# PEER values: dense products with V replaced by one row gather per token and slot

## The reference, cut to what matters

```python
def block(xb):
    ...
    sv, si = lax.top_k(s, PEER_TOPK)
    ...
    e = (i1 * PEER_NKEYS + i2).reshape(T, PEER_HEADS * PEER_TOPK)
    gate = jax.nn.softmax(cv, axis=-1).reshape(T, PEER_HEADS * PEER_TOPK)
    act = jax.nn.gelu(jnp.einsum('ted,td->te', u_tab[e], xb).astype(jnp.float32))
    coef = (gate * act).astype(xb.dtype)
    return jnp.einsum('te,ted->td', coef, v_tab[e])
```

## Time and profile before

| what | us |
|---|---|
| median of three runs | 5477.62 |
| span of the profiled execution | 5473.6 |
| TensorE busy | 5015.2 (92%) |
| VectorE busy | 2899.3 (53%) |
| ScalarE busy | 1068.2 (20%) |
| GpSimd busy | 455.4 (8%) |
| moved by DMA | 476.12 MB, mean 87 GB/s |

### The profile page before, as it was taken

How to read it: one execution, slowest core, us unless ns; L and a number is a source line. 1 busy time by engine, 2 the same in 40 slices (tenths; PEclk the granted TensorE clock), 3 DMA queues, 4 the chain that set the end, 5 groups by cost and what they waited for, 6 DMA issues and landing times. The chain is left out here.

```text
span 5473.6 us, 76074 instructions
## 1 busy us (share of the span) xinstructions
PE 5015.2 (92%) x26871; PEld 4496.7 (82%) x26871; DVE 2899.3 (53%) x7212; ACT 1068.2 (20%) x1825; POOL 455.4 (8%) x328
## 2 busy tenths in 40 slices
PE   7999889998798999988887699999999999999996
PEld 6757888884598999988887688888888899889886
DVE  1021733333315999877776566666644444444444
ACT  2111111111311222222222211111111121112111
POOL 0000033430000000000000022222200000000000
PEclk9999589999799999999989899999999999999998
DMA  3100300002222233244445533333321221121122
GB/s 114 39 23 16 129 23 1 1 1 85 96 70 79 100 105 110 77 134 131 136 131 144 154 141 140 142 142 133 141 76 57 72 72 59 61 72 64 56 72 81
DMA packets 450919, 476.12 MB, mean 87 GB/s; under 512 B 311344, under 2 KB 376240, under 8 KB 449328
## 3 DMA queue, kind: packets, MB, share of 16 engines
q1 hardware_dynamic: 136240, 354.12, 18.6%
q10 hardware_dynamic: 307728, 91.43, 6.2%
q0 software_dynamic: 6768, 28.32, 1.4%
HBM read 336.45 MB, written 137.36 MB: 87 GB/s over the span
## 5 line engine op out<-in xcount | busy, mean ns | idle before, releaser
L1752 DVE TENSOR_TENSOR peer_y<-peer_y,stored_pv 128x512 f32<-128x512 f32 x648 | 443.0, 686 | 271.1 <-PE stored_pv L1781 270.3
L1779 PE MATMUL stored_pv<-stored_Vh,stored_Ch 128*128 128x512 f32 x1296 | 505.5, 390 | 33.1 <-DVE stored_Cl L1738 33.1
L1780 PE MATMUL stored_pv<-stored_Vl,stored_Ch 128*128 128x512 f32 x1296 | 505.2, 390 | 0.0
L1781 PE MATMUL stored_pv<-stored_Vh,stored_Cl 128*128 128x512 f32 x1296 | 505.1, 390 | 0.0
L1952 DVE TENSOR_TENSOR peer_y<-peer_y,experts_pv 128x512 f32<-128x512 f32 x504 | 341.8, 687 | 286.1 <-PE experts_pv L1992 286.1
L1975 PE MATMUL experts_pu<-peer_xh,experts_Uh 128*128 128x384 f32 x1344 | 450.5, 335 | 7.0 <-DVE experts_Ul L1918 7.0
L1977 PE MATMUL experts_pu<-peer_xh,experts_Ul 128*128 128x384 f32 x1344 | 450.2, 335 | 0.0
L1976 PE MATMUL experts_pu<-peer_xl,experts_Uh 128*128 128x384 f32 x1344 | 450.2, 335 | 0.0
L1990 PE MATMUL experts_pv<-experts_Vh,experts_Ch 128*128 128x512 f32 x1008 | 396.1, 393 | 15.1 <-DVE peer_y L1952 12.7
L1599 DVE TENSOR_SCALAR gates_scaled<-gates_iota,retrieve_slotT 128x128 f32<-128x128 f32 x1152 | 396.2, 344 | 0.0
L1991 PE MATMUL experts_pv<-experts_Vl,experts_Ch 128*128 128x512 f32 x1008 | 393.7, 391 | 0.0
(11 more groups left out here) (297 smaller groups left out, 9408.9 us busy)
## 6 DMA issues: line engine op xcount, KB each, us to landing
gates<-gates_G ACTq DMA_DIRECT2D x72, 1024.0 KB, 11.0
stored_C<-acts SPq DMA_DIRECT2D x72, 576.0 KB, 3.8
stored_G<-gates SPq DMA_DIRECT2D x72, 576.0 KB, 4.8
stored_Vr<-in_peer_v SPq DMA_DIRECT2D x72, 512.0 KB, 6.4
experts_G<-gates SPq DMA_DIRECT2D x56, 576.0 KB, 3.8
experts_Ur<-in_peer_u SPq DMA_DIRECT2D x56, 512.0 KB, 5.7
experts_Vr<-in_peer_v SPq DMA_DIRECT2D x56, 512.0 KB, 5.9
acts<-topk_act SPq DMA_DIRECT2D x135, 192.0 KB, 1.9
```

What stands on the lines that cost most here:

```text
L1752: nc.vector.tensor_tensor(dst, dst, pv[r % RING][:], ALU.add).then_inc(y_added, 1)
L1779: mm(pv[r % RING][:], Ch[p][j][:, t], Vh[p][j][:, cols], start=(j == 0), stop=False)
L1780: mm(pv[r % RING][:], Ch[p][j][:, t], Vl[p][j][:, cols], start=False, stop=False)
L1781: last = mm(pv[r % RING][:], Cl[p][j][:, t], Vh[p][j][:, cols], start=False, stop=(j == 1))
```

## The change

The change keeps the picking of experts and makes the activations as before, for all tokens and all 128 blocks: 54 of them in stage_topk (TOPK_AHEAD is 6), and 74 in a new stage, stage_rest, which does nothing else. Each block's activations are stored tile by tile, as nine [128 x 128] pieces, in nine DRAM tensors acts0 to acts8, one word for each expert and token. Gates are no longer spread, and stage_gates, stage_stored and stage_experts go.

A new stage, stage_values, works token by token. It turns the slots of each tile so that a token is a partition, and computes for each token and slot the row of V and the word of its activation. GpSimd then issues, for each of 9 tiles and 128 slots, an indirect DMA that brings one activation for each of 128 tokens (line 1634) and an indirect DMA that brings one row of V of 4 KB for each of 128 tokens (line 1641), into a ring of 12 buffers. The words of a tile are fetched one tile ahead, in turn with the rows. VectorE multiplies activations with gates (line 1674) and adds coefficient times row onto four running sums (lines 1683 and 1686), which it joins at a tile's end (lines 1689 to 1692). At the start of each of tiles 1 to 7 GpSimd waits until VectorE has used all rows issued so far (line 1653). Line numbers here are those of the changed kernel.

```diff
@@ class Ahead
     def store(self, sp, n):
         for c in range(NTC):
             sp.wait_ge(self.gelu_done, 3 * n + (c + 4))
-            sp.dma_start(self.dram["acts"][n + self.first][:, c * TC:(c + 1) * TC], self.act[c][:]).then_inc(self.act_out[c], 16)
+            for t in range(TC // P):
+                dst = self.dram[f"cells{c * (TC // P) + t}"][n + self.first]
+                sp.dma_start(dst, self.act[c][:, t * P:(t + 1) * P]).then_inc(self.act_out[c], 16)
...
-TOPK_AHEAD = 5
-GATE_AHEAD = 3
+TOPK_AHEAD = 6
...
@@ stage_topk, VectorE
-                    if half == 0:
-                        ahead.low(dve, t * A + 4, 4)
+                    ahead.low(dve, t * A + 4 + half, 4 + half)
...
-def stage_gates(core, xh, xl):
...
+def stage_rest(core, xh, xl, first):
+
+    nc = core.nc
+    R = 2
+    LEFT = P - first
...
+        @block.sync
+        def _(sp):
+            ahead.load(sp, 0)
+            with sp.Fori(0, LEFT // R - 1) as i:
+                for b in range(R):
+                    ahead.load(sp, i * R + (b + 1))
+                    ahead.store(sp, i * R + b)
...
         @block.tensor
         def _(pe):
             ahead.begin(pe=pe)
...
+            with pe.Fori(0, LEFT // R) as i:
+                for b in range(R):
+                    for c in range(NTC):
+                        ahead.products(pe, i * R + b, b, c)
...
+def stage_values(core, y):
...
+    RING = 12
+    SUMS = 4
...
+            def gather_act(i, k):
+                pool.indirect_dma_start(act[i % 2][:, k:k + 1], None, dram[f"acts{i}"],
+                                        bass.IndirectOffsetOnAxis(ap=cell[:, i, k:k + 1], axis=0)).then_inc(act_in[i % 2], 16)
+
+            def gather_row(i, k):
+                n = i * SLOTS + k
+                if n >= RING:
+                    pool.wait_ge(v_used, n - RING + 1)
+                pool.indirect_dma_start(V[n % RING][:], None, dram["peer_v"],
+                                        bass.IndirectOffsetOnAxis(ap=row[:, i, k:k + 1], axis=0)).then_inc(v_in[n % RING], 16)
...
+            pool.wait_ge(turned_read, 3)
+            for k in range(SLOTS):
+                gather_act(0, k)
+            for i in range(TILES):
+                if i + 1 < TILES:
+                    pool.wait_ge(turned_read, 3 * (i + 2))
+                    if i >= 1:
+                        pool.wait_ge(v_used, i * SLOTS)
+                for k in range(SLOTS):
+                    if i + 1 < TILES:
+                        gather_act(i + 1, k)
+                    gather_row(i, k)
...
+            for i in range(TILES):
+                dve.wait_ge(act_in[i % 2], 16 * SLOTS * (i // 2 + 1))
+                a = act[i % 2]
+                v.tensor_tensor(a[:], a[:], gate[:, i, :], ALU.mult).then_inc(coef_done, 1)
...
+                for k in range(SLOTS):
+                    n = i * SLOTS + k
+                    total = sums[k % SUMS]
+                    dve.wait_ge(v_in[n % RING], 16 * (n // RING + 1))
+                    if k < SUMS:
+                        v.tensor_scalar(total[:], V[n % RING][:], a[:, k:k + 1], None, ALU.mult).then_inc(v_used, 1)
+                    else:
+                        dve.wait_ge(v_used, n - SUMS + 1)
+                        v.scalar_tensor_tensor(out=total[:], in0=V[n % RING][:], scalar=a[:, k:k + 1], in1=total[:],
+                                               op0=ALU.mult, op1=ALU.add).then_inc(v_used, 1)
+                dve.wait_ge(v_used, (i + 1) * SLOTS)
+                v.tensor_tensor(sums[0][:], sums[0][:], sums[1][:], ALU.add).then_inc(joined, 1)
+                v.tensor_tensor(sums[2][:], sums[2][:], sums[3][:], ALU.add).then_inc(joined, 1)
+                dve.wait_ge(joined, 3 * i + 2)
+                v.tensor_tensor(y[:, i, :], sums[0][:], sums[2][:], ALU.add).then_inc(joined, 1)
...
@@ build
                 stage_topk(core, xh, xl)
-                stage_gates(core, xh, xl)
+                stage_rest(core, xh, xl, TILES * TOPK_AHEAD)
             y = pr.sb("y", [P, TILES, D])
-            made = TILES * (TOPK_AHEAD + GATE_AHEAD)
-            stage_stored(core, y, made)
-            stage_experts(core, xh, xl, y, made)
+            stage_values(core, y)
             stage_final(core, y)
```

More of the change, by code:

```diff
@@ L1552, in _ @@
             turn(TILES - 1)
-def stage_gates(core, xh, xl):
-    nc, dram = core.nc, core.dram
[L1561 to L1578, removed]
+def stage_rest(core, xh, xl, first):
+    nc = core.nc
+    R = 2
+    LEFT = P - first
+    with Stage(core, "rest") as st:
+        ahead = Ahead(core, st, R, first, xh, xl)
+        block = st.block()
+        @block.sync
[5 more added lines that the diff above has]
+                    ahead.store(sp, i * R + b)
+            ahead.load(sp, LEFT - 1)
+            ahead.store(sp, LEFT - 2)
+            ahead.store(sp, LEFT - 1)
+            ahead.stored(sp, LEFT)
+        @block.scalar
+        def _(act):
+            ahead.begin(act=act)
+            ahead.high(act, 0, 0)
+            with act.Fori(0, LEFT // R - 1) as i:
+                for b in range(R):
+                    ahead.high(act, i * R + (b + 1), (b + 1) % R)
+                    ahead.gelu(act, i * R + b)
+            ahead.high(act, LEFT - 1, 1)
+            ahead.gelu(act, LEFT - 2)
+            ahead.gelu(act, LEFT - 1)
+        @block.vector
+        def _(dve):
+            ahead.begin(dve=dve)
+            with dve.Fori(0, LEFT // R) as i:
+                for b in range(R):
+                    ahead.low(dve, i * R + b, b)
+        @block.tensor
+        def _(pe):
+            ahead.begin(pe=pe)
+            with pe.Fori(0, LEFT // R) as i:
+                for b in range(R):
+                    for c in range(NTC):
+                        ahead.products(pe, i * R + b, b, c)
@@ new lines, in stage_values @@
+def stage_values(core, y):
+    nc, dram = core.nc, core.dram
+    RING = 12
+    SUMS = 4
+    with Stage(core, "values") as st:
+        lane = st.sb("lane", [P, 1])
+        expert = st.sb("expert", [P, T])
+        row = st.sb("row", [P, TILES, SLOTS], U32)
+        cell = st.sb("cell", [P, TILES, SLOTS], U32)
+        gate = st.sb("gate", [P, TILES, SLOTS])
+        act = [st.sb(f"act{i}", [P, SLOTS]) for i in range(2)]
+        V = [st.sb(f"V{i}", [P, D]) for i in range(RING)]
+        sums = [st.sb(f"sum{i}", [P, D]) for i in range(SUMS)]
+        pt = [st.psum(f"pt{i}", [P, 2, P]) for i in range(2)]
+        lane_done = st.sem("lane_done")
+        experts_made = st.sem("experts_made")
+        turned, turned_read = st.sem("turned"), st.sem("turned_read")
+        act_in = [st.sem(f"act_in{i}") for i in range(2)]
+        v_in = [st.sem(f"v_in{i}") for i in range(RING)]
+        coef_done = st.sem("coef_done")
+        v_used = st.sem("v_used")
+        joined = st.sem("joined")
@@ L1586, in _ @@
         @block.vector
         def _(dve):
[L1588 to L1600, removed]
+            v = nc.vector
@@ L1602, in _ @@
         @block.tensor
         def _(pe):
[L1604 to L1617, removed]
```

375 lines of the change are left out of this document (36 added, 339 removed).

## The result

The changed kernel takes 6627.19 us (median of four runs, 6620.42 to 6641.75) against 5477.17 us for the kernel before: ratio 1.211 with an interval of 1.209 to 1.212, 21% slower. I had forecast 6210 us, 13% slower. The direction came out as written, and so did the engine that sets the pace, GpSimd; one term of the sum, its price for a gather, was 0.2 us too small, and it stands there 2304 times.

The account below looks back on a forecast made before the run. TensorE bounds the kernel before; in the new stage GpSimd's gathers would set the pace. Dense products and start to 3381 us, plus 2782 us of gathers, plus 45 us last stage: 6208 us, forecast 6210 us, range 5300 to 7200.

Parts of the forecast that it names:

- Dense part: Picking and rest stages: 128 blocks of U at 12.87 us each, 1647 us from 1717.2, ending at 3364.6 us.
- The third rival: Dense stages: nine stores a block break the 12.87 us; losing 3 us a block gives 6590 us; chance 0.05.
- the cover that I named for the nine stores: Dense stages: SyncE issues nine stores and one load in 3.3 of 12.87 us a block, so it has room.
- The price of a gather: Values stage: each indirect DMA holds GpSimd 1.17 us, 2304 of them 2696 us; chance 0.62.
- The second rival: Values stage: GpSimd's gathers and VectorE shut each other out, 3.48 us a slot, 7480 us in all; chance 0.13.
- The first rival: Values stage: gathers cost GpSimd 0.575 us like direct DMAs, the DMA engines set the pace, 5438 us; chance 0.20.
- The DMA engines: Last tile of the values stage: 128 row gathers at 1.50 us (350 GB/s) instead of 1.17 add 42 us.
- The boundaries: Values stage: at seven tile boundaries GpSimd waits for VectorE to use up the tile before, 33 us together.
- the end: After the last gather: last landing and three joins 7 us, then the last stage 45 us.
- the signs that I had listed: Values stage: GpSimd almost gapless, gathers near 1.2 us, line 1686 at 1.3 us and half idle, DMA share about 0.7.

Follow-up runs that it names:

- the phases: Changed kernel with its values stage replaced by four phases of back-to-back gathers (words or rows, 128 or 64 tokens), pauses between, computation with V left out: 5373.44 us.
- sums in PSUM: Changed kernel with three running sums in PSUM instead of four in SBUF: 6621.47 us, ratio to the kernel before 1.2095.
- the run with fewer tokens: Changed kernel with the first tile's word gathers over 128, 64, 32 and 16 tokens and direct DMAs for the last tile's rows: 6595.71 us, single run.

## Why the prediction came out as it did

The sum against the profiled execution of the changed kernel, 6633 us, 423 us above the forecast:

- **Dense part.** 12.87 us a block held in the picking stage (12.84) and was generous in the stage with nothing beside it (12.50). The last dense product starts at 3343 us instead of ending at 3365, and the first gather at 3350.5 instead of 3384.5: -34 us. The third rival is out; the cover that I named for the nine stores was there.
- **The price of a gather**, the term that was too small: 1.17 us. From the first gather to the last start are 3215 us; less 38 us at seven boundaries that is 1.38 us a gather, and 3177 - 2304 x 1.17 = +482 us. I had built it from a direct DMA plus two passes over 128 indices at 2.32 ns a value. The parts were wrong one by one: an index costs 1 ns, the fixed part is 0.82 us instead of 0.54, and there is a gap of 0.30 us that a direct DMA doesn't have. That they add up to 1.25, close by, is luck. The rest, 0.13, is VectorE's hold.
- **The two limits.** In the changed kernel the hold alone makes the mean gather 1.075 us long, 1.38 from start to start, since 860 of its 861 long gathers are held ones. The second limit doesn't come into play: by the account of the phases, against 1.40 us a gather, the lead is 18 us at most in the first two tiles, 14 from there to the last tile and 23 at its end, and the slow pace needs 27 (sums in PSUM) to 30 (phases). With the hold removed the second limit alone gives 6621 us; that this is nearly the same time looks like chance. In the run with fewer tokens, where the first tile was cheaper, both show: 126 of its 934 gathers over 1.0 us are not held ones. At 6371 us it had issued 2176, and (6371 - 3352) / 1.40 = 2156, a lead of 20 gathers, 27 us; the direct DMAs behind were slowed for 27 us.
- **The second rival** was half right, in a way that I had put inside the range ("some tenths of a us a gather"): the hold exists, falls on GpSimd alone, and ends with VectorE's instruction. The Trainium skill has the rule in "SBUF — State Buffer", section "SBUF: two separate sides" (VectorE with two SBUF inputs and a GpSimd operation that reads SBUF share a pair of ports, one at a time). For gathers the traces agree, with 0.94 us against up to 2.0, and 0.95 again with the sums in PSUM; that a gather which starts first holds VectorE in turn, as the rule has it, the trace doesn't show: 1022 of line 1686's instructions start inside a gather and take 1283 to 1287 ns.
- **The first rival** decided below 0.85 us a gather. Nothing here came near it, since even 16 tokens cost 1.14.
- **The DMA engines.** I took 350 GB/s and added 42 us for the last tile; it ran at 404 GB/s and the term was not there: -42 us.

```profile
6411.00:6566.00 155.00, 0.00 (x0) 0.00 (x0) 150.49 (x120) 0.00 (x0) 118.44 (x121) 0.50 1.02 404
```

- **The boundaries** cost 38 us instead of 33, 7 times and at most 5.6 us, as worked out, and the end 66 us instead of 52. -34 + 482 - 42 + 5 + 14 = 425, of 423.

```profile
POOL values_act L1634 <- DVE values_sum L1686: 38.1, 7, 5.6
```

Of the signs that I had listed, line 1686 at 1.28 us and idle half the time and a DMA share of 0.63 against 0.7 came out. GpSimd is never free, but it isn't busy almost without a gap: 2476.8 of 3230 us, 77%, with 0.30 us behind each gather; and lines 1634 and 1641 take 1.00 and 1.15 us on average instead of near 1.2 both.

What stays open is what the second limit is. That gathers slow to 1.40 us whatever their tokens and bytes once a lead of 27 to 30 us is used up, that a pause gives it back, and that their data land as soon as before all the same, is shown; what stands behind it no run here tells.

## What to carry to other kernels

Price a gather by its count: here 1.25 us of GpSimd for each, 1.38 on average beside VectorE instructions with two inputs in SBUF, 1.40 where more than some 150 to 220 follow each other without a pause, and almost nothing for its bytes or its tokens, so bring everything that a token needs in one gather. With 8 KB for both rows instead of a word and a row, the time from the first gather to the last falls from 3215 to 2899 us, although VectorE does two instructions a slot there; the other 1137 of the 1449 us less come from the dense products left out, since gathers begin at 2214 us instead of 3350.5. When a wait is taken away and the time stays, compare the pace in the first microseconds of the stage with that in its middle; a second limit that needs time to fill shows only there. And an engine that looks idle by nature, like GpSimd at 8% before, has to be priced for each instruction that a change hands to it.

## What the hardware showed unexpectedly

- Gathers slow to 1.40 us each after 153 to 216 in a row, though the last of 400 words had landed 1.42 us after its gather's end; direct DMAs that follow are slowed for 27 us, while direct DMAs alone run at 0.55 us, 600 in a row.
- GpSimd's gather waits for VectorE's instructions with two SBUF inputs, 0.94 us becoming up to 2.0, and VectorE never for a gather (1287 ns at most in 1022); a direct DMA from the same engine doesn't wait (537 ns median, 606 at most, 116 of the 128 started inside such an instruction).
- One core gathered rows at random addresses at 404 GB/s with 4 KB rows and at 416 GB/s with 8 KB rows.
